# Attention over three branches in one stream of batches: query tiles alternating, latent preparation on two PSUM banks

## The reference

```python
def hybrid_layer(x, ...):                      # x: [1, 256, 1024]; twice, with their own weights
    z = rmsnorm(x, mix_norm) @ w_in            # a_q, a_kc, ... b_q, b_k, b_v, c_cq, c_ckv, c_kpe
    o_a = nsa_attention(...)                   # 8 heads: selected + window + compressed keys, gated sum
    o_b = swa_sink_attention(...)              # 8 heads: a band of 128 keys, with sinks
    o_c = mla_attention(c_cq, c_ckv, ...)      # 8 heads: the latent branch
    merged = g_a * (o_a @ w_branch_a) + g_b * (o_b @ w_branch_b) + g_c * (o_c @ w_branch_c)
    x = x + merged @ w_out
    ...                                        # feed-forward part

def compress_blocks(t, tok, pos, w1, w2):      # keys and values of the compressed attention
    return jax.nn.gelu(flat @ w1) @ w2         # flat: 15 windows of 32 tokens

def mla_attention(cq, ckv, k_pe_raw, q_norm, w_q_up, kv_norm, w_kv_up, cos32, sin32):
    q = (rmsnorm(cq, q_norm) @ w_q_up).reshape(B, S, 8, 96)      # 64 without, 32 with rotation
    kv = (rmsnorm(ckv, kv_norm) @ w_kv_up).reshape(B, S, 8, 128) # 64 of keys, 64 of values
    ...
    return causal_block_attention(qf, kf, v, 96 ** -0.5)

# each attention: p = softmax(mask(q @ k.T * scale)); out = p @ v
```

## Time and profile before

| | us |
|---|---|
| median of 3 executions (lowest, highest) | 3016.33 (3015.28, 3019.54) |
| the profiled execution | 3015.33 |
| its span, first to last instruction | 3013.5 |
| attention phase, first layer | 153.4 to 238.5 |
| attention phase, second layer | 660.9 to 746.2 |

### The profile page before, as it was taken

One profiled execution on the slowest core, in us unless ns is written; L12 is line 12 of the kernel. 1 busy time (PEld: TensorE's weight loads), 2 busy tenths in 40 slices (PEclk: granted clock), 3 DMA queues, 4 the chain that ended last, 5 costly groups with the idle time before them and its releaser, 6 DMA issues. The chain is left out here.

```text
span 3013.5 us, 35585 instructions
## 1 busy us (share of the span) xinstructions
PE 2568.0 (85%) x13094; PEld 1875.1 (62%) x13094; DVE 2111.5 (70%) x4120; ACT 1087.6 (36%) x1979; POOL 607.1 (20%) x575
## 2 busy tenths in 40 slices
PE   8999999998999899898977666668999897666666
PEld 7968997886998797797542222226888653222222
DVE  6477655557765574646888888866674799888876
ACT  4374444447444465444221111114654222112111
POOL 0000000000000000001445444440000354444442
PEclk9999999999999999999998888889999998888888
DMA  6423554441555333345999999996433899999997
GB/s 259 173 99 141 185 182 168 165 176 58 185 183 195 146 127 112 112 156 210 415 424 426 426 427 427 426 427 278 154 125 135 357 425 421 426 426 427 426 427 309
DMA packets 112493, 810.80 MB, mean 269 GB/s; under 512 B 12736, under 2 KB 12736, under 8 KB 14272
## 3 DMA queue, kind: packets, MB, share of 16 engines
q0 software_dynamic: 73728, 536.90, 42.4%
q1 hardware_dynamic: 38592, 271.63, 24.8%
HBM read 807.44 MB, written 1.05 MB: 268 GB/s over the span
## 5 line engine op out<-in xcount | busy, mean ns | idle before, releaser
L3515 PE MATMUL ps<-arena 128*128 128x512 f32 x912 | 519.5, 721 | 245.2 <-ACT arena L3411 232.8
L167 DVE TENSOR_TENSOR ring_low<-ring,parts 128x2048 fp32r<-128x2048 f32 x214 | 488.0, 2291 | 311.6 <-ACT parts L161 308.0
L480 PE MATMUL ps<-parts,parts 128*128 128x256 f32 x2528 | 570.0, 283 | 2.5 <-PEq L393 1.7
L3515 PEld LDWEIGHTS ps<-arena 128*128 128x128 f32 x912 | 200.4, 229 | 550.2 <-ACT arena L3411 309.9
L480 PE MATMUL ps<-parts,ring_low 128*128 128x256 f32 x1824 | 512.1, 281 | 0.0
L161 ACT ACTIVATE parts<-ring 128x2048 fp32r<-128x2048 f32 x214 | 406.8, 1913 | 275.7 <-PE ps L488 106.2
L488 PE MATMUL ps<-parts,parts 128*128 128x512 f32 x1344 | 439.2, 396 | 5.8 <-DVE ring_low L167 3.8
L480 PEld LDWEIGHTS ps<-parts,parts 128*128 128x128 f32 x2528 | 428.3, 189 | 3.7 <-issue 2.1
L3238 POOL DMA_INDIRECT arena<-in_experts,stage_index x276 | 319.9, 1159 | 531.5 <-PE ps L3515 233.8
L3515 PE MATMUL ps<-ring,arena 128*128 128x512 f32 x616 | 314.3, 647 | 103.9 <-ACT arena L3411 100.1
L3286 DVE CUSTOM_DVE_ANT_0 arena<-arena 128x1024 f32<-128x1024 f32 x276 | 334.0, 1228 | 96.6 <-DMA arena<-in_experts,stage_index 93.8
(11 more groups left out here) (506 smaller groups left out, 2941.2 us busy)
## 6 DMA issues: line engine op xcount, KB each, us to landing
ring<-in_stream SPq DMA_DIRECT2D x249, 1024.0 KB, 4.8
arena<-in_experts,stage_index POOLq DMA_INDIRECT x276, 22.6
ring<-in_experts,stage_index POOLq DMA_INDIRECT x236
gain_row<-in_gain_rows SPq DMA_DIRECT2D x4, 512.0 KB, 5.9
arena<-in_mem SPq DMA_DIRECT2D x2, 1024.0 KB, 4.7
arena<-in_stream SPq DMA_DIRECT2D x2, 1024.0 KB, 8.4
par<-in_params SPq DMA_DIRECT2D x4, 386.0 KB, 4.6
x<-in_x SPq DMA_DIRECT2D x1, 1024.0 KB, 5.2
```

The lines of the kernel that those rows point to most:

```text
L167: dve.tensor_tensor(k.ring_low[v % SLOTS], whole, self.high_of(v).bitcast(F32), ALU.subtract).then_inc(self.ph.sem("chunk_split"), 1)
L480: last = pe.matmul(self.ps[:, 2 * pair + f // 2, (f % 2) * T:(f % 2 + 1) * T], w[:, f * P:(f + 1) * P], x[:, k, :], start=(k == 0 and i == ...
L3515: last = pe.matmul(k.ps[:, bank + n, :], diag[:, s % ROWS, :], rows[row_of[s]][:, D + n * BLK:D + (n + 1) * BLK], start=(s % SLOTS_PER_TOK ...
```

## The change

The list of batches now goes through the query tiles in its innermost loop, so short and long alternate: batches 0, 2, 4, ... 10 are short and 1, 3, 5, ... 11 long. The compressed and latent batches stay where they were.

The ups go to other slots: the query ups to slots 0, 2 and 4, the key ups to 5, 6, 8 and 9. Ups 3 and 6 use bank 7, all others bank 5. The compression's second product goes from slot 6 to slot 7. The head turns go to slots 10 to 14: one each in slots 10 and 11, then two per slot, one ahead of the turn and one at the slot's end; head turns 2, 4 and 6 use bank 5. ACT takes the first two, DVE the other six.

Since long turns and ups in bank 5 now alternate, there are more waits on PE: every long turn from 1 to 9 waits for the take of the up before it, and each up in bank 5 (after the first) waits for the copy of the long turn before it.

```diff
         def up_bank(i):
-            return shared if i < 5 else spare
+            return spare if i in (3, 6) else shared
         def turn_bank(i):
-            return shared if i in (4, 6) else spare
+            return shared if i in (2, 4, 6) else spare
...
                 def turn(b):
-                    if b == 6:
-                        pe.wait_ge(ph.sem("up_copied"), 5)
+                    if b in (1, 3, 5, 7, 9):
+                        pe.wait_ge(ph.sem("up_copied"), (1, 2, 3, 5, 6)[b // 2])
...
                 def query_up(i):
                     if i >= 1:
                         pe.wait_ge(ph.sem("up_copied"), i)
+                        pe.wait_ge(ph.sem("probs_turned_copied"), 2 * i)
...
                 def key_up(i):
-                    if i < 5:
-                        pe.wait_ge(ph.sem("up_copied"), i)
+                    if i == 3:
+                        pe.wait_ge(ph.sem("hidden_taken"), 1)
+                    if i == 4:
+                        pe.wait_ge(ph.sem("up_copied"), 3)
+                        pe.wait_ge(ph.sem("probs_turned_copied"), 6)
                     if i == 5:
-                        pe.wait_ge(ph.sem("hidden_taken"), 1)
+                        pe.wait_ge(ph.sem("up_copied"), 5)
+                        pe.wait_ge(ph.sem("probs_turned_copied"), 8)
...
                 def compress():
-                    pe.wait_ge(ph.sem("up_copied"), 6)
+                    pe.wait_ge(ph.sem("up_copied"), 4)
...
                 def turn_heads(i):
-                    elif i < 4:
+                    elif i < 3:
                         pe.wait_ge(ph.sem("c_copied"), i)
-                    elif i > 4:
+                    else:
                         pe.wait_ge(ph.sem("c_copied"), i - 1)
+                    if i == 2:
+                        pe.wait_ge(ph.sem("probs_turned_copied"), 12)
...
                 for b in range(nb):        # PE
-                    if 1 <= b <= 3:
-                        query_up(b - 1)
-                    if 4 <= b <= 5:
-                        key_up(b - 1)
-                    if 12 <= b <= 13:
-                        turn_heads(2 * b - 21)
+                    if b in (0, 2, 4):
+                        query_up(b // 2)
+                    if b in (6, 8):
+                        key_up(b // 2 + 1)
+                    if 12 <= b <= 14:
+                        turn_heads(2 * b - 22)
                     turn(b)
...
                     if b == 5:
-                        key_up(5)
-                    if b == 6:
+                        key_up(3)
+                    if b == 7:
                         compress()
-                    if b == 8:
+                    if b == 9:
                         key_up(6)
-                    if 9 <= b <= 11:
-                        turn_heads(b - 9)
-                    if 12 <= b <= 13:
-                        turn_heads(2 * b - 20)
-                    if b == 14:
-                        turn_heads(7)
+                    if 10 <= b <= 11:
+                        turn_heads(b - 10)
+                    if 12 <= b <= 14:
+                        turn_heads(2 * b - 21)
...
-    batches = [batch(kind, pair, m) for m in range(MT) for pair in range(2) for kind in ("selected", "window", "band")]
+    batches = [batch(kind, pair, m) for pair in range(2) for kind in ("selected", "window", "band") for m in range(MT)]
```

More of the change, by code:

```diff
@@ L1452, in _ @@
                         hidden_gelu()
-                    if b == 7:
+                    if b == 8:
                         take_compressed()
-                    if 12 <= b <= 13:
+                    if 12 <= b <= 14:
+                        take_heads(2 * b - 22)
                         take_heads(2 * b - 21)
-                        take_heads(2 * b - 20)
-                    if b == 14:
-                        take_heads(7)
                 out(nb - 2)
@@ L1528, in _ @@
                 for b in range(nb):
[L1529 to L1534, removed]
+                    if 11 <= b <= 12:
+                        take_heads(b - 11)
+                    if b in (0, 2, 4):
+                        take_query(b // 2)
+                    if b == 6:
+                        take_key(3)
+                    if b in (6, 8):
+                        take_key(b // 2 + 1)
                     if b == 5:
@@ L1537, in _ @@
                         act.activation(hid2, hid2, ACT.Exp, scale=-1.5957691216057308).then_inc(ph.sem("hidden_exp"), 1)
-                    if b == 9:
+                    if b == 10:
                         take_key(6)
```

## The result

| | before | after |
|---|---|---|
| median of 20 executions each, us (lowest, highest) | 3016.54 (3014.91, 3021.93) | 3021.64 (3017.66, 3026.87) |
| the profiled execution, us | 3015.33 | 3022.41 |
| attention phase, first and second layer, us | 85.1, 85.3 | 89.6, 89.6 |

The ratio is 1.0015, with a 95% interval of 1.0009 to 1.0021: the change makes the kernel slower, by less than the 0.2% that I called "no change". I had forecast 3013.9, a saving of 2.4 us, in a range up to 3018.3. The measured median lies above the range: the change costs 5.1 us where I had it save.

A forecast was written before the change was run, and what follows sets the result against it. TensorE bounds each attention phase's first 69.0 us, VectorE the tail. TensorE waits fall from 4.7 to 3.5 us per layer, saving 2.4 in two: 3012.9 profiled, median 1.0 above, 3013.9 us; range 3009.5 to 3018.3.

The forecast's parts named there:

- Slot 0: First round of the batch loops: query_up(0) ahead of turn(0) covers TensorE's 1.3 us wait for VectorE's scale, which goes.
- Slots 6 to 10: With short and long batches alternating, VectorE keeps ahead of TensorE; waits for the scale go from 1.9 us to 0.
- Slot 12: turn_heads(2) waits for both ScalarE head copies: 1.4 us instead of 0.83, ends 0.9 and 1.9.
- Slots 13 and 14: VectorE takes six head groups instead of five; TensorE's waits at these turns total 0.3 us, ends 0 and 0.6.
- The fences: Waits between long turns and ups sharing bank 5 cost nothing, unless ScalarE runs more than 1.4 us late.
- rival 2: Bank 5 waits bite, three of them 0.4 us late per layer: 3016.3 us, no change; chance 0.10.
- Slots 4 and 5: New TensorE wait at turn(5), behind turn_hidden and VectorE's hidden_cubes and scale(5): 1.8 us, at most 2.2.
- What else moves: Side effects, such as GpSimd's query rotation starting some 4 us later, wanted only over 20 us on: no cost.
- The clock: No drop to half clock in the phase's first 69 us; tails may each come out 0.7 us either way.
- rival 3: Waits in slots 5 or 12 halve TensorE's clock, about 1.7 us each; both, both layers: 3020.7 us; chance 0.08.
- The time within "no change": Whole kernel's time counts as the same within 0.2%, 3010.3 to 3022.4 us; chance of same 0.83.
- The forecast's own range: Whole kernel: saving of 0 to 4.0 us and tails 0.7 each, 3010.5 to 3017.5; chance 0.70.

The follow-up runs named there:

- the rotation late: Changed kernel with GpSimd's rotation of the queries also waiting for VectorE's hidden_gelu: median 3013.20 us, ratio 0.9991.
- The combined kernels: Changed kernel with rotation behind hidden_gelu and key_up(3) ahead of turn(5): 3011.42 us; with head copies also counted on two semaphores: 3008.94; that with rotation behind batch 7's scale: 3009.38.
- all three edits together: Changed kernel with GpSimd's rotation behind hidden_gelu, key_up(3) ahead of turn(5), and ScalarE's and VectorE's head copies on separate semaphores: 3008.94 us, ratio 0.9974.

## Why the prediction was wrong, point by point

**Slot 0: right.** The wait is gone; turn(0) came at 159.52, and I had 159.4.

**Slots 6 to 10: right.** No wait is left there, so TensorE and not VectorE sets the pace of the alternating pairs, as I had argued; with the rotation late and the clock at 1.00 throughout there is none either. The combined kernels show how thin the slack is: with the key_up moved ahead of turn(5) and GpSimd on the scale of batch 6, waits of 0.56 and 0.64 came back.

**Slot 12: right.** 1.31 us, where I had 1.4 with ends of 0.9 and 1.9. **Slots 13 and 14: right,** 0.19 against 0.3. **The fences: right.** No up waits for bank 5 (none of L1243, L1247 and L1267 is in the wait table), so rival 2 falls.

**Slots 4 and 5: wrong by 2.4 us.** The mechanism was the one I named; the size was 4.16 where I had 1.8 and "at most 2.2". The step that failed stands further down in the prediction: "What else moves" puts GpSimd's rotation 4 us later and costs it at nothing, because its result is wanted only 20 us on. I asked who waits for it and not what it now runs beside. Its new place is exactly the chain from turn_hidden to turn(5), and there it stretches VectorE's instructions with operands in SBUF. With the rotation out of the way the wait was 1.75, and the phase took 67.1 us up to the scores of batch 18, where my sum gives 69.0 - 1.2 = 67.8: the rest of the sum was right to 0.7 us per layer. That the median of 3013.2 meets the forecast of 3013.9 as closely is in part luck, since I had the tails with their half clock, and in that profile they had none.

The Trainium skill has a rule for this, which I had not weighed for a step that I took as free. "SBUF — State Buffer", under "Who interferes with whom", says that VectorE and GpSimd share one pair of ports as an exclusive lock: a VectorE instruction with two inputs in SBUF contends with a GpSimd instruction that reads SBUF, and one with at most one SBUF input does not, unless it is of a kind that can run in a two-port mode, such as tensor_scalar. The trace agrees row by row: tensor_tensor 0.83 against 0.28 and tensor_scalar 0.63 against 0.22, while the copy from PSUM stays at 0.28. The reciprocal at 182.79 says little, since GpSimd paused from 182.74 to 182.91; that of the kernel before, at 176.17, lies wholly within one of GpSimd's multiplications and took 0.18.

**The clock: wrong.** I took no drop in the first 69 us, and gave 0.08 to rival 3, which is what happened in its full form: both waits, both layers. I had priced a stretch at 1.7 us. In the profiled execution TensorE's busy time grew by 4.2 us per layer in two stretches of 6.8 and 3.4 us at half clock; a stretch of 3.4 costs up to the 1.7 that I took from the tails, and one of 6.8 up to twice that; TensorE was not busy in all of it. By layer the balance against my forecast of 83.9 is: waits 5.66 - 3.5 = 2.2, clock 4.2, tail 15.5 - 16.1 = -0.6, sum 5.8, and 83.9 + 5.8 = 89.7. Rival 3 had 3020.7 for this case, near the measured 3021.64, but not by its own terms: it took a wait of 1.8 and 1.7 us for each stretch, and kept the tails as they were.

The first error made the second: with a wait of 1.75 the clock stayed at 1.00 in both layers, the level that I had taken for a wait between the 1.3 and the 2.1 us of my rows.

**The time within "no change".** The bound of 0.2% was kept, but the range was too short at its upper end, since it left out the case with both waits in both layers. The forecast's own range of 3010.5 to 3017.5 is added up wrongly, too: a saving of 0 to 4.0 and 0.7 for each tail give 3010.9 to 3017.7. Nothing else hangs on it.

## What to carry to other kernels

When a change moves a step of an engine that nobody waits for, look at what runs beside its new place, not only at when its result is wanted; a GpSimd step that works on SBUF belongs over VectorE work that reads PSUM, or where VectorE is idle. A wait of TensorE like those of 2.2 us and more here, in the midst of dense work, is not priced by its length: put the half clock behind it into the sum (2.5 us of added wait cost 7.1). And where two operations count on one semaphore, the order of the queue they are on becomes a wait for whoever needs only the other; but taking that one wait away gave nothing by the median here, and all three edits together 7 to 8 us against the kernel before, so look at the waits together.

## What the runs showed of the hardware

**Half clock behind waits.** Over the two layers of twelve profiles the counts are:

| wait of TensorE | layers with it | clock fell behind it |
|---|---|---|
| turn(5), 4.1 to 4.3 us | 8 | 8 (five for 6.8 us, three for 3.4) |
| turn(5), 3.0 us | 2 | 2 (6.8 and 3.4) |
| turn(5), 2.2 us | 2 | 2 (3.4 both) |
| turn(5), 1.6 to 1.75 us | 4 | 0 |
| head turn of slot 12, 1.3 us | 14 | 5 (3.4 each) |
| first long wait of the tail, 2.1 us | 20 | 7 (3.4 each) |

Four more falls stand in tails behind a wait of only 0.53 us, two of them for 6.8 us. So at turn(5), in the dense part, the clock fell behind each of the 12 waits of 2.2 us or more; in the sparser stretches the length of the last wait doesn't decide. The five falls in slot 12 are in five of the six layers where the clock had been down for 6.8 us behind turn(5) and slot 12 had its wait; of the eight other layers with that wait none fell. A link between the two, or a common cause, is likely by these counts; no run tests it, and what sets 3.4 or 6.8 stays open. The Trainium skill, "TensorE: Matmul & The Clock Gate", under "HAM oscillation — how this bites in real kernels", has idle gaps between bursts bring the clock down, in a kernel whose gaps are some 3 to 5 us long. The trace agrees for the waits of 3.0 us and more at turn(5); here waits of 2.2 us were enough too, and the four of 1.6 to 1.75 us left the clock at 1.00.

**VectorE beside GpSimd.** The loss is a wait of some 0.4 to 0.55 us per instruction and not a slower rate: 0.28 became 0.83 and 0.16 became 0.68, but 1.22 became only 1.60. Each of GpSimd's multiplications takes 0.73 us, so short VectorE instructions came to stand in step with them, one for one. By these rows, many small instructions are the dearest thing to lay beside such a step. Who pays is a matter of hundredths of a us: in the changed kernel GpSimd began at 179.75 and VectorE at 179.79, and VectorE took 0.83 instead of 0.28; in the kernel before VectorE began first, at 176.74 against 176.76, and GpSimd took 1.25 instead of 0.73.
